# Retention sample states in a hybrid decoder step: updated by VectorE from a broadcast row instead of by outer products on TensorE

## The reference

```
s = s * chunk_decay + einsum('bhjd,bhjv->bhdv', kc * tail, vc)   # s: 256 x 512, k: 256, v: 512
o = einsum('bhid,bhdv->bhiv', qc, new s)                         # o: 512
```

## Time and profile before

| | |
|---|---|
| median of 3 runs | 4340.7 us |
| the profiled execution | 4343.53 us; span from first to last instruction 4342.0 us |
| busy share of the span | PE 80%, DVE 57%, POOL 48%, ACT 16% |
| mean granted TensorE clock | 0.944 of full speed |
| retention heads | about 198 to 200 us each, four of them |
| L1761 `outer` | 128 instructions in the trace, 63.3 us busy |
| L1770 `state_out` | 128 instructions in the trace, 60.3 us busy |

### The profile page before, as it was taken

The page is one execution under the profiler, slowest core; times in us unless marked ns, Lnnn a source line. Parts: engine busy times, 40 slices in busy tenths (PEclk is TensorE's granted clock), DMA queues, the critical chain, the costliest instruction groups (busy, mean ns, idle before and its releaser), DMA issues.

```text
span 4342.0 us, 31227 instructions
## 1 busy us (share of the span) xinstructions
PE 3477.0 (80%) x9454; PEld 1403.5 (32%) x9454; DVE 2466.6 (57%) x5878; ACT 688.6 (16%) x1660; POOL 2091.6 (48%) x2201
## 2 busy tenths in 40 slices
PE   6898999999777777776877874997777777777777
PEld 1333333335322222222322343454222232232222
DVE  3314242333966677687764448139766676778643
ACT  2201101011111111111211132110111111111111
POOL 1110100001677776777776500005777767777765
PEclk8799999999899999999999987998999999999999
DMA  9831313222899999999999825318999999999998
GB/s 335 277 116 49 130 58 117 73 87 105 325 409 410 409 409 396 399 409 403 396 407 409 317 54 97 109 43 312 409 409 409 409 396 401 409 401 396 409 409 323
DMA packets 405204, 1285.44 MB, mean 296 GB/s; under 512 B 49550, under 2 KB 73262, under 8 KB 404015
## 3 DMA queue, kind: packets, MB, share of 16 engines
q0 software_dynamic: 309312, 1126.31, 66.3%
q1 hardware_dynamic: 95560, 155.13, 11.3%
q10 hardware_dynamic: 180, 2.18, 0.1%
HBM read 1254.67 MB, written 28.79 MB: 296 GB/s over the span
## 4 chain that ended last, share of the span: by engine, by line
PE 32%; DMA 23%; POOL 19%; DVE 15%; issue 8%; ACT 2%; SPq 1%; POOLq 0%; DVEq 0%; ACTq 0%
DMA w<-in_peer_u_dram,arena 12%; POOL arena L1335 10%; DMA arena<-in_peer_v_dram,arena 10%; POOL w L1335 9%; PE ps L1742 8%; PE ps L1919 4%; DVE w L2284 3%; PE ps L1841 3%; DVE arena L2284 3%; PE ps L1888 3%; PE ps L798 3%; DMA w<-in_w_ada_dram 2%; PE ps L1761 1%; PE ps L1770 1%; PE ps L690 1%
## 5 line engine op out<-in xcount | busy, mean ns | idle before, releaser
L1919 PE MATMUL ps<-arena 128*128 128x512 f32 x3944 | 1947.0, 623 | 639.6 <-DMA arena<-in_peer_v_dram,arena 550.8
L2284 DVE CUSTOM_DVE_ANT_0 w<-w,ps 128x1024 f32<-128x1024 f32 x896 | 1090.1, 1218 | 697.7 <-DMA w<-in_peer_u_dram,arena 696.1
L1919 PEld LDWEIGHTS ps<-arena 128*128 128x128 f32 x3944 | 693.2, 192 | 1868.8 <-DMA arena<-in_peer_v_dram,arena 1213.7
L1335 POOL DMA_INDIRECT arena<-in_peer_v_dram,arena x1040 | 995.2, 957 | 431.1 <-issue 251.9
L1335 POOL DMA_INDIRECT w<-in_peer_u_dram,arena x912 | 865.7, 949 | 280.2 <-issue 238.9
L1573 ACT ACTIVATE arena<-ident,arena 128x128 f32<-128x128 f32 x986 | 377.2, 398 | 1613.4 <-PE ps L1919 1588.6
L1742 PE MATMUL ps<-w,hT 128*128 128x512 f32 x768 | 345.0, 603 | 0.0
L1888 PE MATMUL ps<-hT,w 128*128 128x512 f32 x512 | 275.7, 631 | 1.5 <-ACT hT L1415 1.5
L1296 POOL DMA_DIRECT2D out_dram<-arena x32 | 23.4, 730 | 520.8 <-DVE arena L2053 376.8
L1335 POOL DMA_INDIRECT arena<-in_peer_u_dram,arena x128 | 125.1, 977 | 222.2 <-DVE arena L2216 122.3
L1742 PEld LDWEIGHTS ps<-w,hT 128*128 128x128 f32 x768 | 143.7, 192 | 202.9 <-issue 199.4
(11 more groups left out here) (312 smaller groups left out, 2951.4 us busy)
## 6 DMA issues: line engine op xcount, KB each, us to landing
w<-in_w_ada_dram SPq DMA_DIRECT2D x32, 1024.0 KB, 11.6
w<-in_ret_w_in_dram SPq DMA_DIRECT2D x24, 1024.0 KB, 7.2
out_dram<-arena POOLq DMA_DIRECT2D x36, 512.0 KB, 3.3
arena<-in_peer_v_dram,arena POOLq DMA_INDIRECT x1040, 10.7
x<-in_w_ada_dram SPq DMA_DIRECT2D x16, 1024.0 KB, 11.6
arena<-in_state_ret_dram POOLq DMA_DIRECT2D x32, 512.0 KB, 5.0
w<-in_peer_w_q_dram SPq DMA_DIRECT2D x16, 1024.0 KB, 7.3
w<-in_peer_u_dram,arena POOLq DMA_INDIRECT x912, 11.1
```

What stands on the lines that cost most here:

```text
L1335: pool.indirect_dma_start(ring[:, slot, :], None, table, bass.IndirectOffsetOnAxis(ap=index, axis=0)).then_inc(landed_sem[slot], 16)
L1919: mm = pe.matmul(ps[:, bank + half, :], diag[:, n % DIAGS], v_ring[:, n % RING, half * BW:(half + 1) * BW], start=(n % NE == 0), stop=(n % ...
L2284: dve.tensor_tensor_reduce(row, row, h_ps, 1.0, 0.0, ALU.mult, ALU.add, acts[:, j % 2, s:s + 1]).then_inc(u_used, 1)
```

## The change

- The outer products leave PE. The samples' values of the head (8 x 512) are written to a small DRAM tensor `v_d` by SP, and read back as one row broadcast to 128 partitions: `vb`, three slots of 128x512 (256 KB for each sample). Their semaphores are three existing ones (`w_ld[2]`, `x_ld`, `p1_ld`).
- PE transposes the samples' keys as well as queries (four small transposes instead of two); ACT copies the keys to `kcol`, so that each partition holds its key value.
- DVE scales the state by the decay (a tensor_scalar over 128x1024), then adds `vb * kcol` in two pieces of 128x512, all in SBUF. `kz` is gone.
- `state_out(b)` writes 32 rows instead of 8, into column group 2 * (b % 2) + c of bank 4, with c the half of the state; the four groups are added after the last projection group by `sample_sum(4)`, one more small matmul, from a copy that ACT makes.

```diff
+            def v_broadcast(b):
+                sp.dma_start(vb[:, b % 3, :], v_d[b:b + 1].to_broadcast([P, DV])).then_inc(vb_ld[b % 3], 16)
             def head_blocks(head, last):
                 sp.wait_ge(y_done, head * 2 * TILES + 1)
                 load_block(1, columns(1, ret_w_in[0], head * DV + 2 * HEADS * DK))
+                sp.wait_ge(proj_done, head * HEAD_GROUPS + HEAD_PLACE[1, TP] + 1)
...
+                sp.dma_start(v_d, proj[0:NS, TP, BW:2 * BW]).then_inc(v_st, 16)
+                sp.wait_ge(v_st, head * 16 + 16)
...
+                for b in range(3):
+                    v_broadcast(b)
                 sp.wait_ge(proj_ps, head * HEAD_GROUPS + HEAD_PLACE[0, 3] + 1)
                 load_block(0, columns(0, ret_w_in[0], head * DV + 2 * HEADS * DK + HEADS * DV))
+                for b in range(3, NS):
+                    sp.wait_ge(s1_done, head * NS + b - 2)
...
+                    v_broadcast(b)
                 sp.wait_ge(proj_ps, head * 3 * TILES + 2 * TILES)
                 load_block(1, out_rows(1, head))
```

```diff
                 for n, (j, t) in enumerate(HEAD_ORDER):
                     rows = ROWS[t]
+                    if n == HEAD_GROUPS - 1:
+                        act.wait_ge(os_ps, head * (NS + 1) + NS)
+                        act.activation(head_sums, ps[:, 4, :], ACT.Copy).then_inc(part_done, 1)
```

```diff
-                    for c in range(2):
-                        mm = pe.transpose(ps[:, 7, c * NS:(c + 1) * NS], qkr[0:NS, TP, 0, c * P:(c + 1) * P],
+                    for c in range(4):
+                        mm = pe.transpose(ps[:, 7, c * NS:(c + 1) * NS], qkr[0:NS, TP, c // 2, c % 2 * P:(c % 2 + 1) * P],
                                           ident[0:NS, 0:NS])
...
-                def outer(b):
...
                     for c in range(2):
-                        mm = pe.matmul(ps[0:NS, 4, :], qz[:, c, b * NS:(b + 1) * NS], sring[:, b % 2, c],
-                                       start=(b == 0 and c == 0), stop=(b == NS - 1 and c == 1))
+                        j = 2 * (b % 2) + c
+                        mm = pe.matmul(ps[32 * j:32 * j + 32, 4, :], qz[:, c, b * NS:b * NS + 32], sring[:, b % 2, c],
+                                       start=(b < 2), stop=(b >= NS - 2))
...
                 sample_query()
-                outer(0)
                 for b in range(NS):
                     n = HEAD_PLACE[0, 3] + b
                     group(n)
-                    if b + 1 < NS:
-                        outer(b + 1)
                     state_out(b)
                 for n in range(HEAD_PLACE[0, 3] + NS, HEAD_GROUPS):
                     group(n)
+                pe.wait_ge(part_done, head * 4 + ADA_BLOCKS + 4)
+                sample_sum(4, head_sums).then_inc(os_ps, 1)
```

```diff
                     dve.wait_ge(s0_ld[b % 2], head * (NS // 2) * 16 + 16 * (b // 2 + 1))
-                    dve.wait_ge(outer_ps, head * NS + (b + 1))
+                    link.link(dve.tensor_scalar(sring[:, b % 2], sring[:, b % 2], cols[:, 3:4], None, ALU.mult))
+                    if b == 0:
+                        dve.wait_ge(kcol_done, head + 1)
+                    at, per_head = vb_landed(b)
+                    dve.wait_ge(vb_ld[b % 3], head * per_head + at)
                     for c in range(2):
-                        ins = dve.scalar_tensor_tensor(sring[:, b % 2, c], sring[:, b % 2, c], cols[:, 3:4],
-                                                       ps[:, 2 + c, :], ALU.mult, ALU.add)
+                        ins = dve.scalar_tensor_tensor(sring[:, b % 2, c], vb[:, b % 3], kcol[:, c, b:b + 1],
+                                                       sring[:, b % 2, c], ALU.mult, ALU.add)
                     ins.then_inc(s1_done, 1)
...
-                dve.wait_ge(os_ps, head * NS + NS)
+                dve.wait_ge(os_ps, head * (NS + 1) + NS + 1)
```

More of the change, by code:

```diff
@@ L170, in build @@
         z_d = nc.dram_tensor("z_d", (TP * P + NS, D), F32).ap()
+        v_d = nc.dram_tensor("v_d", (NS, DV), F32).ap()
         k_d = nc.dram_tensor("k_d", (G, GP, 2 * BL - 1, GP), F32).ap()
@@ L209, in build @@
         kt = cut(TP, DK)
[L210 to L211 removed]
+        vb = cut(3, DV)
+        kcol = cut(2, NS)
+        qz = cut(2, NS * NS + 32 - NS)
+        head_sums = cut(BW)
         sring = cut(2, 2, DV)
@@ L288, in build @@
         s1_st = [sem("s1_st0"), sem("s1_st1")]
-        outer_ps, s1_done, os_ps = sem("outer_ps"), sem("s1_done"), sem("os_ps")
+        v_st, s1_done, os_ps = sem("v_st"), sem("s1_done"), sem("os_ps")
         g_tanh, og_done, oT_ps, oT_done = sem("g_tanh"), sem("og_done"), sem("oT_ps"), sem("oT_done")
@@ L419, in build, with vb_landed @@
         p1_ld, p2_ld, h2_ld = sem("p1_ld"), sem("p2_ld"), sem("h2_ld")
+        vb_ld, vb_ld_from = [w_ld[2], x_ld, p1_ld], [32 * ADA_SLOTS.count(2), 32, 48]
+        def vb_landed(b):
+            return vb_ld_from[b % 3] + 16 * (b // 3 + 1), 16 * len(range(b % 3, NS, 3))
         kzero_st, ud_st, ub_zero = sem("kzero_st"), sem("ud_st"), sem("ub_zero")
@@ L1300, in head_states @@
                         pool.wait_ge(s1_st[slot], head * (NS // 2) * 16 + 16 * ((b - 1) // 2 + 1))
-                        pool.wait_ge(os_ps, head * NS + b)
+                        pool.wait_ge(os_ps, head * (NS + 1) + b)
                         pool.sem_inc(issued, 1)
@@ L1308, in head_states @@
                     pool.wait_ge(s1_st[1], head * (NS // 2) * 16 + 16 * (NS // 2))
-                    pool.wait_ge(os_ps, head * NS + NS)
+                    pool.wait_ge(os_ps, head * (NS + 1) + NS)
                     pool.sem_inc(issued, 1)
@@ L1737, in group @@
                     if t == TP:
-                        pe.wait_ge(part_done, head * 3 + ADA_BLOCKS + j + 1)
+                        pe.wait_ge(part_done, head * 4 + ADA_BLOCKS + j + 1)
                         mm = sample_sum(6, head_sums)
@@ L1748, in sample_query @@
                     pe.sem_inc(issued, 1)
-                    for c in range(2):
-                        mm = pe.transpose(ps[:, 7, c * NS:(c + 1) * NS], qkr[0:NS, TP, 0, c * P:(c + 1) * P],
+                    for c in range(4):
+                        mm = pe.transpose(ps[:, 7, c * NS:(c + 1) * NS], qkr[0:NS, TP, c // 2, c % 2 * P:(c % 2 + 1) * P],
                                           ident[0:NS, 0:NS])
                     mm.then_inc(qk_ps, 1)
-                def outer(b):
-                    if b == 0:
-                        pe.wait_ge(kz_done, head + 1)
-                        pe.wait_ge(proj_done, head * HEAD_GROUPS + HEAD_PLACE[1, TP] + 1)
-                    else:
-                        pe.wait_ge(s1_done, head * NS + b)
-                    for c in range(2):
-                        mm = pe.matmul(ps[:, 2 + c, :], kz[:, b, c * P:(c + 1) * P],
-                                       proj[0:NS, TP, BW:2 * BW], start=True, stop=True)
-                    mm.then_inc(outer_ps, 1)
                 def state_out(b):
```

18 lines of the change are left out of this document (10 added, 8 removed).

## The result

The changed kernel takes **4311.1 us** (median of 4 runs, 4306.9 to 4313.1) against 4340.9 us for the kernel before (4 runs, 4339.5 to 4342.6). The ratio is 0.993, with a 95% interval from 0.9913 to 0.9947. That is 30 us less where 55 were predicted, and 2 us above the range. The profiled execution took 4306.92 us, its span is 4305.3 us, the mean granted clock 0.943.

What follows compares the result with a forecast made beforehand. The prediction took state loads, no longer PE, to bound each changed head: 15.0 us gained, less 1.2 for the clock, leaves 13.8, times 4 = 55 us, so 4340.7 - 55 gives 4285 us; range 4266 to 4309.

Steps and rivals of the forecast that it cites:

- What goes from PE: Retention heads: outer products gone, `state_out` 0.95 instead of 1.81 us, less added transposes and sum: net 21.6 us a head.
- The state chain becomes the bound: State updates in each head: state loads end last, period 8.74 us against PE's 8.01; 15.0 us a head gained.
- The round trip through DRAM: Head start: samples' values stored and broadcast back, covered by group (0, 3) with 0.3 us to spare.
- I add 1.5 us in all for it: States 2 to 7: delay of state loads meeting weight loads or broadcasts, 1.5 us, between nothing and 3.8.
- run beside state loads today without any load of the loop showing in a wait: Argument about 1 MB weight loads, landing in 7.2 us, against the rival that the kernel gets slower, 4373 us, chance 0.05.
- The clock: After PE's new 5 us wait: one group 1.7 us longer at the lower clock, 1.2 us a head lost.
- the rival: After PE's new wait: 1.2 GHz for 13.7 us of dense work, 6.4 us a head lost, 4306 us; chance 0.08.
- The other edits are free: DVE's later end work, ACT's copies, moved load positions and dropped `kz` in each head: no cost, no gain.
- the transfers are slow: State loops: broadcasts delay each load by 0.64 us, the first lands in 6.8; 30 us gained, 4311 us; chance 0.12.
- No overlap: `state_out`: column groups do not overlap, PE's pitch 8.9 us, 1 to 2 us a head lost, 4290 us; chance 0.05.
- PE stays the bound: State loops: loads bring the period under 8.0 us, all 21.6 us a head come through, 4254 us; chance 0.08.

Runs made afterwards that it cites:

- the last two versions: Changed kernel with both weight loads late and the short sample group behind sample 7: 4242.8 us; the same with POOL's load ahead of its store: 4237.3 us.
- the control: Kernel before the change, outer products on PE, with w_out's load behind state 7 and the short sample group behind sample 7: 4338.4 us.
- the last version: Changed kernel, both weight loads late, short sample group behind sample 7, POOL issuing the load of state b+1 ahead of the store of state b: 4237.3 us.

## Why the prediction was wrong

*What goes from PE* was right. `state_out` is 0.98 instead of the forecast 0.95, and where PE waits for nothing (the last two versions, but for the 0.69 us) the stretch to the transposes is 102.0 and 101.3 us in the third head, 21.2 and 21.9 below 123.2, for a forecast 21.6. That the column groups alone gave 25 us for a forecast 24 was luck: 13.9 of it lie in this stretch.

*The state chain becomes the bound* was right, and so was its period: 8.74 forecast, 8.53 and 8.61 for the last two states. The round trip through DRAM too: from the end of ACT's copy (608.94) to the end of update 0 (615.47) 6.53 us, forecast 6.5, and state 1 is 4.3 us behind it, forecast 4.4. Within the round trip there was luck: the broadcast took 3.46 us for a forecast 2.8, and the store and the two issues made up for it.

*The step that failed* is "I add 1.5 us in all for it", for the loads that meet a weight load or a broadcast. From the end of one update to the end of the next, states 2 to 7 took 12.0, 9.0, 9.0, 14.8, 8.5 and 8.6 us, 61.9 in all, where the step had 52.4 + 1.5. It is 9.5 in place of 1.5: 3.3 at state 2 and 6.1 at state 5, little at the others. The runs with one or both weight loads moved give 27, 10 and 34 us back, so their part is shown. With both moved the six periods take 54.6 us, and without the five broadcasts as well 51.4 (scalings at 597.06 and 648.49): the weight loads are 7.3 us a head and the broadcasts 3.2, where the step had 1.5 for both.

The bound was drawn from the wrong transfer. I put the 410 GB/s of the earlier trace rows to the broadcast's 256 KB and stopped there. By the same row a weight load's 2 MB need 5.1 us of all the DMA engines, and there are two in a head: 10.2 us by this estimate, 7.3 measured. That I left them out rested on "run beside state loads today without any load of the loop showing in a wait": a wait that did not show since PE's pitch was 10.78 us, and a distance of 4.65 us that the change itself took away. The warning stood in the 11.2 us of the earlier trace rows: in the kernel before SP issued a weight load of the first head at 197.03, POOL two state loads from 197.41 on, and these landed after 10.1 and 11.2 us; nothing needed them soon. The Trainium skill ("DMA: Bandwidth & Descriptors", Issuing engines are not separate DMA queues), which I had quoted for the broadcasts alone, says it for all transfers; the 11.04 and 7.79 us of POOL's transfers beside SP's loads agree.

*The clock* was half right. The fall comes in every head and lasts 13.5 to 13.7 us, as the rival had it; the Trainium skill ("TensorE: Matmul & The Clock Gate", HAM oscillation) says the same of a PE that waits for transfers, and the granted clock of 0.50 in all four heads (281.9 to 295.5, 473.0 to 486.6, 664.2 to 677.8, 851.9 to 865.6) agrees. Half of that stretch is waiting, so it costs 8.51 - 7.13 for a group and 0.9 for a `state_out`, of which 1.73 us show (update 7 ends at 681.74, its `state_out` starts at 683.47); I took 1.2.

Together: 8.0 us of transfers and 0.5 of clock are 8.5 us a head, and the third head's stretch is 117.9 where 123.2 - 13.8 = 109.4 was forecast. Over the four heads the stretch gave 23.5 us, and a head as a whole takes 189 to 194 us where 184 were forecast.

*The other edits are free* was too low, by a gain. `sample_sum(4)` hides ACT's last copy, and the short fall of the clock behind it went: 7.4 us over the four heads. With 23.5 that is 30.9, for a measured 30; the spans of the two traces differ by 36.7, so some 6 us between them lie outside these stretches. The run with the column groups alone has this gain too (22.2 us in three heads, 21.8 in the last), so it comes with the sum. The part of it that is clock is not sure in each execution: in the control, without the sum, one head of four shows the fall, where the kernel before had three.

Of the rivals, "the transfers are slow" had the time, 4311, but only part of the cause: the broadcasts do set back a load by 0.4 to 1.1 us, for its 0.64, but the first broadcast landed in 3.46 us, not 6.8, and the weight loads are not in it. "No overlap" gave 4290, 5 us over the forecast; undoing the overlap cost 1 us, so that argument held though its premise didn't. "PE stays the bound" came about once the loads had been moved: 4254 worked out, 4237 to 4243 measured, lower by more than the 7.4 us above. In the last version the four stretches are 91.1 us shorter than before, for the 86 of this rival; with the 7.4 that is 98.5 of the 104, and the last 6 us stay open.

## What to carry to other kernels

When a change moves the bound from an engine to a transfer, write down every transfer of every queue in that stretch and price its bytes at the measured rate, the large old ones first: that they didn't show before may only mean that a slower engine covered them. Two edits that each shorten the engine in front don't add up once the next chain sets the pace: in the stretch that they share they gave 13.9 and 17.2 us alone, 23.5 together. Moving two loads and one short group brought out 99 us; two of these three moves were tried in the old kernel, where they are worth nothing that can be measured. Put long independent work ahead of a wait and short work behind it.

## What the runs showed of the hardware

A state load of 512 KB that goes out 0.7 us behind 2 MB on another queue lands after 11.0 us instead of 4.6 to 5.3 (third head of the changed kernel; 10.0 to 11.0 in the four heads), and a store of that size that goes out with them after 7.8 and 9.1 instead of 3.2 to 4.3. Over such a meeting the DMA engines moved 299 and 304 GB/s on the average (windows: us; busy times; PEclk; DMA share, GB/s):

```profile
616.30:624.00 7.70, 7.70 (x20) 3.10 (x20) 5.44 (x13) 0.26 (x2) 1.42 (x2) 1.00 0.90 299
651.30:662.30 11.00, 8.39 (x28) 3.07 (x18) 0.00 (x0) 1.19 (x2) 0.69 (x1) 1.00 0.86 304
```

That average is not the rate at which they are full: from 651.3 to 656 they moved 226 GB/s, from 656 to 661 it was 423, a little above the 410 of the expert layers.

A row of 2 KB broadcast to 128 partitions (256 KB) landed in 3.1 to 4.0 us with no weight load in flight, about as long as a store of twice the bytes (3.2 to 4.3); the one of each head that went out 1.2 us behind the start of the gate columns' load took 10.0 to 11.3.
